# GpSimd computes the norm of the differential heads' outputs; VectorE keeps its sums over heads

## Chip, cores and metric

The kernel runs on one core of one Trainium2 chip. The metric is the device time of one execution in microseconds. The profile names the engines PE (TensorE matmul), DVE (VectorE), ACT (ScalarE), POOL (GpSimd) and SP (SyncE, here the DMA queue for weights).

## What is computed

Two transformer blocks of two layers each on 256 tokens of width 1024. The change lies in the attention of the first block, which runs once for each of its two layers. That layer has four kinds of heads; one of them, the differential heads, ends with a norm over each head's 64 outputs:

```python
def rmsnorm(x, g):
    xf = x.astype(jnp.float32)
    y = xf * lax.rsqrt(jnp.mean(xf * xf, axis=-1, keepdims=True) + EPS)
    return (y * g.astype(jnp.float32)).astype(x.dtype)
...
    out = from_blocks(lax.map(one_block, (to_blocks(q), jnp.arange(nb))))
    return rmsnorm(out, subln_g) * (1.0 - lam_init)
...
    mix = jnp.concatenate([o_a.reshape(b, s_len, -1), o_b.reshape(b, s_len, -1),
                           o_c.reshape(b, s_len, -1), o_d.reshape(b, s_len, -1)], axis=-1)
    x = x + rmsnorm(mix @ w_out, g_post_mix)
```

So the normed outputs of the differential heads (`o_c`) are a part of the left side of the product with `w_out`.

## The kernel before

Every engine has a program of its own, written out by hand in the order in which it shall run, and the engines meet at semaphores. The helpers `do` (DVE) and `step` (POOL) let an engine wait for each of its own instructions before the next one. All matmuls are made as three products of high and low parts of the operands, so each tile of weights that SP loads into `ring` gets a high part from ACT (`ring_hi`, L1652) and a low part from DVE (`ring_lo = ring - ring_hi`, L2166, or in two halves, L2174). The function `met` on DVE and ACT is where such a part is made.

The 256 tokens are two blocks of 128, `tb` 0 and 1. The attention of a layer is ten units, `u` 0 to 9: for each block c0, c1 (the differential heads, two and two), d (sliding), b (forgetting), a (selected keys). For a unit PE makes the logits two units ahead (`logits`, L1026, L1033, L1036), DVE the maxima (`maxima`, L2413 to L2418), ACT the exponentials (`exps`, L1739), PE transposes the probabilities (`prob_transposes`, L720 from ARENA) and ACT copies them out of PSUM (L1729), PE multiplies with the values (`values`, L1060), and DVE weighs the result into `XN` (`out`, L2444, L2445 or L2447), which raises the semaphore `o_ready`. The tile `SM` of the profile holds all small tensors (`ms8`, `r8`, `p_sub` and others), `ARENA` the scratch tensor `SQC`.

Behind unit c1 (u = 1 and 6) DVE's function `between` squares the four differential heads' 128x256 outputs, sums each head's 64 squares and adds the epsilon (L2452, L2453, L2454). POOL raises the four means to the power -1/2 (`asked`, L3048, 128x4). One unit later (u = 2 and 7) DVE multiplies the outputs by the root and by the gain `p_sub` (L2459, L2460) and raises `cd_ready`.

PE uses these outputs in `output_transposes(tb, 1)`, four transposes of `XN` columns 512 to 1023 (L720 from XN), which wait for `cd_ready`: for block 0 in unit 3, ahead of `last_columns(3, 1)` (the last products of the input projection), and for block 1 in unit 8, ahead of `values(8)`. ACT and DVE then split the transposed outputs (L1678, L2193), and `out_rows` multiplies them with `w_out`. In `between`, DVE also makes the selection mask (`choose`, L2367 to L2373) and in units 2 and 4 the low part of a weight tile.

POOL has little other work. At the start of the stage it rotates the heads c and d for both blocks (L3083 to L3086, L3117), then loads a gain vector (`gains`, a DMA issue, L3091), serves the two powers, and later serves the norms of the layer (L3052, L3048).

Of the kernel before, what the change touches and what calls it, by code (L numbers as in the profile page):

```python
# [12 lines left out]
ALU = mybir.AluOpType  # L13
ACT = mybir.ActivationFunctionType
AX_X = mybir.AxisListType.X

P = 128
D = 1024
S = 256  # L20
NTB = S // P
KT = D // P
DEPTH = 2
EPS = 1e-6
BIG = 1e30
TAKEN = -3e38
HD = 64
# [107 lines left out]
def build(nc, at, n_const, const_d, w, out_d):  # L135
    ctx = ExitStack()

    def sb(name, shape, dt=F32):
        return ctx.enter_context(nc.sbuf_tensor(name, shape, dt))

    def sig(name):
        return Signal(ctx.enter_context(nc.semaphore(name)))
# [24 lines left out]
    XN = sb("XN", [P, NTB, D])  # L167
# [22 lines left out]
    def c(name):  # L190
        o, n = at[name]
        return C[:, o:o + n]
# [4 lines left out]
    def small(n):  # L197
        o = small_at[0]
        small_at[0] += n
        assert small_at[0] <= 900  # L200
        return SM[:, o:o + n]
# [4 lines left out]
    p_sub = small(128).rearrange("p (l d) -> p l d", l=2)  # L206
# [16 lines left out]
    ms8, r8 = small(8), small(8)  # L223
# [4 lines left out]
    def ar(o, n):  # L228
        assert o + n <= ARENA_N, (o, n)
        return ARENA[:, o:o + n]  # L230
# [16 lines left out]
    SQC = ar(o + 896, 256)  # L247
# [131 lines left out]
    dstep, astep, pstep = sig("dve_step"), sig("act_step"), sig("pool_step")  # L379
    a2d, d2a = sig("act_to_dve"), sig("dve_to_act")  # L380
    d2p, p2d = sig("dve_to_pool"), sig("pool_to_dve")
# [5 lines left out]
    pv_done, o_ready = sig("pv_ready"), sig("o_ready")  # L387
# [5 lines left out]
    in_half = sig("last_columns_first_block")  # L393
    mask_made = sig("selection_mask")
    cd_ready = sig("differential_and_sliding_outputs")
    idx_s, idx_taken = sig("index_dots"), sig("index_dots_taken")
    silu_ready, hb_ready = sig("silu_ready"), sig("hidden_ready")
    h_full, h_side = sig("hidden_half_full"), sig("hidden_low_products_copied")
# [24 lines left out]
    def step(eng, ins, s):  # L423

        ins.then_inc(s.sem, 1)
        s.made += 1
        eng.wait_ge(s.sem, s.made)
# [169 lines left out]
    NU = len(UNITS)  # L597
# [33 lines left out]
    def half_bank(tb, half):  # L631

        return T[0] if half == 0 else G[:, 1, :] if tb else Sp[:, 0, :]
# [16 lines left out]
    def _(pe):  # L650
# [63 lines left out]
        def transposes(i, pairs, parts=False, act_takes=False, other=False):  # L714

            if not other:
                bank_free_t(i)
            for dst, src in pairs:
                k = src.shape[0]
                last = pe.transpose(dst, src, ident[0:k, 0:k])  # L720
            n = n_x if parts else n_p if act_takes else n_t
            n[i] += 1
            t_free[i] = (x_taken[i] if parts else p_taken if act_takes else t_taken[i], n[i])
            last.then_inc((x_full[i] if parts else p_full if act_takes else t_full[i]).sem, 1)
# [186 lines left out]
        for l in range(DEPTH):  # L911
# [151 lines left out]

            def output_transposes(tb, half):
                if half:
                    pe.wait_ge(cd_ready.sem, NTB * l + tb + 1)
                else:
                    pe.wait_ge(o_ready.sem, NU * l + NU // 2 * (tb + 1))
                bank = half_bank(tb, half)
                other = half == 1  # L1070
                kept = t_free[0]
                transposes(0, [(bank[:, k * P:(k + 1) * P], XN[:, tb, (4 * half + k) * P:(4 * half + k + 1) * P]) for k in range(4)], parts=True,
                           other=other)
                if other:
                    half_taken.append(t_free[0])
                    t_free[0] = kept
# [27 lines left out]
            for u in range(NU):  # L1104
                tb = UNITS[u][2]
# [142 lines left out]
        for l in range(DEPTH):  # L1248
# [99 lines left out]
            for lv in range(1, LEVELS):  # L1348
# [21 lines left out]
                if lv <= NTB:  # L1370

                    tb = lv - 1
# [255 lines left out]
        for h in range(2):  # L1628
            pe.wait_ge(z_l.sem, h + 1)
            cs = slice(h * 512, (h + 1) * 512)  # L1630
# [519 lines left out]
    def _(dve):  # L2150
        v = nc.vector
# [3 lines left out]
        def do(ins, s=None):  # L2155

            step(dve, ins, s or dstep)
# [21 lines left out]
        def met(n, ahead=H - 1):  # L2179

            n_use["dve"] += n
            low_parts(n_use["dve"] + ahead)
# [150 lines left out]
        for l in range(DEPTH):  # L2333
# [112 lines left out]
                else:  # L2446
                    do(v.tensor_tensor(dst, src, weights_, ALU.mult), o_ready)  # L2447

            def sublayer_squares(tb):
                oc = XN[:, tb, 512:768]  # L2450
                cs = slice(4 * tb, 4 * tb + 4)
                do(v.tensor_tensor(SQC, oc, oc, ALU.mult))  # L2452
                do(v.tensor_reduce(ms8[:, cs], SQC.rearrange("p (h n) -> p h n", h=4), AX_X, ALU.add))  # L2453
                do(v.tensor_scalar(ms8[:, cs], ms8[:, cs], 1.0 / HD, EPS, ALU.mult, ALU.add), d2p)  # L2454

            def sublayer_norm(tb):
                dve.wait_ge(p2d.sem, p2d.next("dve"))
                oh = XN[:, tb, 512:768].rearrange("p (h d) -> p h d", h=4)
                do(v.tensor_tensor(oh, oh, r8[:, 4 * tb:4 * tb + 4].unsqueeze(2).to_broadcast([P, 4, 64]), ALU.mult))  # L2459
                do(v.tensor_tensor(oh, oh, p_sub[:, l, :].unsqueeze(1).to_broadcast([P, 4, 64]), ALU.mult), cd_ready)  # L2460

            def low_evac_half(half, tb):
                ks, toks = slice(4 * half, 4 * half + 4), slice(tb * P, (tb + 1) * P)
                low_evac(0, xTl[:, ks, toks], xTh[:, ks, toks], half_bank(tb, half))

            def between(u):
                if u in (1, 6):
                    sublayer_squares(u // 5)
                if u in (2, 7):
                    sublayer_norm(u // 5)  # L2470
                if u == 3:
                    low_evac_half(1, 0)
                if u in LOW_AT:
                    met(1, LEAD)
                if u < len(CHOOSE_AT) and CHOOSE_AT[u]:
                    choose(1, sum(CHOOSE_AT[:u]), sum(CHOOSE_AT[:u + 1]))
# [138 lines left out]
        for l in range(DEPTH):  # L2615
# [148 lines left out]
            for lv in range(1, LEVELS):  # L2764
# [13 lines left out]
                if 2 <= lv <= NTB + 1:  # L2778

                    tb = lv - 2  # L2780
                    t0()
                    src = T[0][:, :].rearrange("p (h d) -> p h d", h=4)
                    cs = slice(4 * tb, 4 * tb + 4)
# [4 lines left out]
                if 3 <= lv <= NTB + 2:  # L2788

                    tb = lv - 3  # L2790
# [217 lines left out]
        for h in range(2):  # L3008
            cs = slice(h * 512, (h + 1) * 512)
# [31 lines left out]
    def _(pool):  # L3041
        g = nc.gpsimd
# [4 lines left out]
        def power(dst, src, n, s):  # L3047
            g.tensor_tensor(dst, src, c("mhalf")[:, 0:n], ALU.pow).then_inc(s.sem, 1)  # L3048
# [25 lines left out]
        def asked(dst, src, n, s_in=d2p, s_out=p2d):  # L3074
            pool.wait_ge(s_in.sem, s_in.next("pool"))
            power(dst, src, n, s_out)
# [11 lines left out]
        def gains(q, name, l):  # L3088

            vec_loaded[q].made += 16  # L3090
            pool.dma_start(VEC[:, q, :], w[name][l].partition_broadcast(P)).then_inc(vec_loaded[q].sem, 16)  # L3091

        def gains_loaded(q):
            pool.wait_ge(vec_loaded[q].sem, vec_loaded[q].made)
# [5 lines left out]
        for l in range(DEPTH):  # L3100
            if l:
                gains_loaded(1)
                rms()

                gains(0, "norm_post_mix", l)

            def rotated(col, heads, width, tb, s=None):
                cos, sin = (RCOS32, RSIN32) if width == 32 else (RCOS, RSIN)
                n = heads * width  # L3110
                rope(PROJ[:, tb, col:col + n], cos[:, tb, :], sin[:, tb, :], heads, width, XN[:, 1, 0:n], XN[:, 1, 256:256 + n], s)

            def sliding(tb):
                rotated(D_Q, 4, 64, tb)
                rotated(D_K, 2, 64, tb)
                for q, col in enumerate((D_K, D_K + 64)):
                    last = g.tensor_copy(IKD[:, 1 + q, tb, :].rearrange("p (r d) -> p r d", r=2),  # L3117
                                         PROJ[:, tb, col:col + 64].unsqueeze(1).to_broadcast([P, 2, 64]))
                last.then_inc(d_rotated.sem, 1)

            def differential(tb):
                rotated(C_Q, 8, 32, tb)
                rotated(C_K, 8, 32, tb, c_rotated)

            pool.wait_ge(g_act.sem, l * G_ACT + 10)
            differential(0)
            pool.wait_ge(g_act.sem, l * G_ACT + 11)
            sliding(0)
            differential(1)
            pool.wait_ge(g_act.sem, l * G_ACT + 13)  # L3130
            sliding(1)

            gains(1, "norm_pre_mlp", l)
            for tb in range(NTB):
                asked(r8[:, 4 * tb:4 * tb + 4], ms8[:, 4 * tb:4 * tb + 4], 4)
            for q in range(2):
                gains_loaded(q)
            rms_behind_rms()

            gains(0, "norm_post_mlp", l)  # L3140
            load(PLE, w["p"][l, 0].rearrange("(t p) d -> p t d", p=P), misc_loaded)
            gains_loaded(0)
            rms()

            gains(1, *(("norm_pre_mix", l + 1) if l + 1 < DEPTH else ("ln1_b_2", 0)))
            if l == DEPTH - 1:
                load(WSA, w["a_ws_2"][0].rearrange("g t s -> t g s"), misc_loaded)
        for l in range(DEPTH):
# [10 lines left out]
            for tb in range(NTB):  # L3159
                pool.wait_ge(o_ms.sem, o_ms.next("pool"))  # L3160
                cs = slice(4 * tb, 4 * tb + 4)
# [68 lines left out]
```

## Time and profile before

| | us |
|---|---|
| median of 3 runs | 2010.65 (2010.52 to 2013.17) |
| the profiled execution | 2010.38 |
| its span, first to last instruction | 2008.6 |
| PE busy | 1977.7 |
| DVE busy | 1582.2 |
| ACT busy | 1215.8 |
| POOL busy | 98.4 |

The profiled execution's own time is 1.8 us above its span. The stage of the change is 95 to 145 us from the span's start in layer 0, and ends at 497 in layer 1. A bracket at the end of a row of the timeline tells how long the engine was idle before that row, and which instruction's end let it go on.

### The profile page before, as it was taken

To read this page: it belongs to the slowest core of one execution; us is meant where nothing else is said; L and a number is where in the kernel's file an instruction comes from. 1 tells how busy PE (TensorE), PEld (TensorE's weight loads), DVE (VectorE), ACT (ScalarE), POOL (GpSimd) and SP (SyncE) were. 2 spreads that over 40 slices of the span, in tenths; PEclk is the share of its full clock that TensorE was granted. 3 is DMA by queue.
4 is the path that set the end of the run, shared out by engine and by line. 5 is a ranking of instruction groups with operands and counts; after the bars stand their busy time and mean duration, and the time that the engine had idled before them with its cause. 6 is when DMAs were issued, how large, how long until landed. Compare 5 with 4: busy or idle time off the path is not lost.

```text
span 2008.6 us, 30332 instructions
## 1 busy us (share of the span) xinstructions
PE 1977.7 (98%) x11699; PEld 1677.9 (84%) x11699; DVE 1582.2 (79%) x1634; ACT 1215.8 (61%) x1303; POOL 98.4 (5%) x163
## 2 busy tenths in 40 slices
PE   8999999999999999999999999999999999999997
PEld 7878888887888898888889888888888888888886
DVE  7787745778774569775548978999999998989997
ACT  6565534556553456544436636777777777777775
POOL 0300000030000000000000000000000000000000
PEclk9999999999999999999999999999999999999999
DMA  8326555632655554065556309999999999999995
GB/s 303 117 74 215 192 195 181 207 125 72 214 192 196 187 200 154 17 220 183 189 168 210 106 1 372 362 362 371 359 364 366 358 367 363 366 363 364 366 361 200
DMA packets 154088, 481.06 MB, mean 240 GB/s; under 512 B 14608, under 2 KB 41728, under 8 KB 153856
## 3 DMA queue, kind: packets, MB, share of 16 engines
q1 hardware_dynamic: 150064, 465.46, 64.1%
q0 software_dynamic: 3920, 14.16, 2.0%
q8 instruction: 73, 1.20, 0.2%
q14 instruction: 31, 0.25, 0.0%
HBM read 477.48 MB, written 2.10 MB: 239 GB/s over the span
## 4 chain that ended last, share of the span: by engine, by line
PE 89%; DVE 7%; ACT 2%; issue 1%; DMA 1%; POOL 0%; SPq 0%; DVEq 0%; POOLq 0%; ACTq 0%
PE G L693 18%; PE G L695 18%; PE G L694 18%; PE Sp L695 5%; PE Sp L693 5%; PE Sp L694 5%; PE G L1179 3%; PE G L720 3%; PE G L1180 2%; PE G L680 1%; DVE ring_lo L2166 1%; PE G L675 1%; PE G L676 1%; PE Sp L1179 1%; PE G L1567 1%
## 5 line engine op out<-in xcount | busy, mean ns | idle before, releaser
L2089 ACT ACTIVATE e_hi<-e_raw 128x1408 fp32r<-128x1408 f32 x384 | 523.4, 1380 | 156.9 <-DMA e_raw<-in_moe_w_gate 60.3
L2945 DVE TENSOR_TENSOR e_lo<-e_raw,e_hi 128x1408 fp32r<-128x1408 f32 x384 | 601.3, 1619 | 19.6 <-ACT e_hi L2089 17.2
L2166 DVE TENSOR_TENSOR ring_lo<-ring,ring_hi 128x2048 fp32r<-128x2048 f32 (+2 forms) x171 | 383.4, 2253 | 181.8 <-ACT ring_hi L1652 180.4
L1652 ACT ACTIVATE ring_hi<-ring 128x2048 fp32r<-128x2048 f32 (+1 forms) x179 | 335.4, 1882 | 228.9 <-PE G L695 137.1
L693 PE MATMUL G<-e_hi,xgTh 128*128 128x512 f32 (+1 forms) x768 | 289.2, 377 | 0.1
L695 PE MATMUL G<-e_hi,xgTl 128*128 128x512 f32 (+1 forms) x768 | 288.5, 376 | 0.0
L694 PE MATMUL G<-e_lo,xgTh 128*128 128x512 f32 (+1 forms) x768 | 287.1, 374 | 0.0
L693 PE MATMUL G<-ring_hi,xT 128*128 128x512 f32 (+2 forms) x488 | 190.9, 391 | 0.0
L695 PE MATMUL G<-ring_hi,xT 128*128 128x512 f32 (+2 forms) x488 | 187.4, 384 | 0.0
L694 PE MATMUL G<-ring_lo,xT 128*128 128x512 f32 (+2 forms) x488 | 187.2, 384 | 0.0
L694 PEld LDWEIGHTS G<-e_lo,xgTh 128*128 128x128 f32 x768 | 144.2, 188 | 23.9
L695 PEld LDWEIGHTS G<-e_hi,xgTl 128*128 128x128 f32 x768 | 144.0, 188 | 23.0
L693 PEld LDWEIGHTS G<-e_hi,xgTh 128*128 128x128 f32 x768 | 144.3, 188 | 22.6 <-DVE e_lo L2945 0.4
L693 PE MATMUL Sp<-e_hi,hEh 128*128 128x512 f32 x352 | 138.4, 393 | 0.0
L695 PE MATMUL Sp<-e_hi,hEl 128*128 128x512 f32 x352 | 137.4, 390 | 0.0
L694 PE MATMUL Sp<-e_lo,hEh 128*128 128x512 f32 x352 | 137.2, 390 | 0.0
L693 PEld LDWEIGHTS G<-ring_hi,xT 128*128 128x128 f32 x488 | 91.6, 188 | 19.3 <-issue 1.8
L695 PEld LDWEIGHTS G<-ring_hi,xT 128*128 128x128 f32 x488 | 91.6, 188 | 18.2
L694 PEld LDWEIGHTS G<-ring_lo,xT 128*128 128x128 f32 x488 | 91.7, 188 | 17.4 <-issue 0.5
L1179 PE MATMUL G<-xT,ring_hi 128*128 128x512 f32 x288 | 100.8, 394 | 0.0
L693 PE MATMUL G<-ring_hi,hTh 128*128 128x512 f32 x256 | 100.0, 391 | 0.0
L695 PE MATMUL G<-ring_hi,hTl 128*128 128x512 f32 x256 | 99.7, 389 | 0.0
(463 smaller groups left out, 3370.5 us busy)
## 6 DMA issues: line engine op xcount, KB each, us to landing
e_raw<-in_moe_w_gate SPq DMA_DIRECT2D x128, 704.0 KB, 6.0
e_raw<-in_moe_w_up SPq DMA_DIRECT2D x128, 704.0 KB, 6.0
e_raw<-in_moe_w_down SPq DMA_DIRECT2D x128, 704.0 KB, 6.0
ring<-in_w_in SPq DMA_DIRECT2D x48, 1024.0 KB, 4.9
ring<-in_w_mlp_up SPq DMA_DIRECT2D x32, 1024.0 KB, 5.1
ring<-in_w_mlp_down SPq DMA_DIRECT2D x32, 1024.0 KB, 4.8
ring<-in_w_out SPq DMA_DIRECT2D x16, 1024.0 KB, 4.8
ring<-in_ffn_w_gate SPq DMA_DIRECT2D x22, 512.0 KB, 3.6
```

The source lines that it names most:

```text
L675: pe.matmul(out, ah, bh, start=start, stop=False, **kw)
L676: return pe.matmul(out, al, bh, start=False, stop=False, **kw)
L693: pe.matmul(out, ah, bh, start=start, stop=False, **kw)
L694: pe.matmul(out, ah, bl, start=False, stop=False, **kw)
L695: return pe.matmul(out, al, bh, start=False, stop=stop, **kw)
L720: last = pe.transpose(dst, src, ident[0:k, 0:k])
L1179: pe.matmul(out.rearrange("p (w s) -> p w s", w=2), bh[:, k, ms_], xT[:, :, kk, :], start=kk == 0, stop=False, skip_group_check=True)
L1180: last = pe.matmul(out[:, 0:S], bl[:, k, ms_], xTh[:, kk, :], start=False, stop=kk == KT - 1, skip_group_check=True)
L1652: nc.scalar.activation(ring_hi[:, n % H, 0:m], ring[:, n % R, 0:m], ACT.Copy).then_inc(w_hi.sem, 1)
L2089: nc.scalar.activation(e_hi[:, u, :], e_raw[:, u, :], ACT.Copy).then_inc(w_hi.sem, 1)
L2166: v.tensor_tensor(ring_lo[:, n % R, cs], ring[:, n % R, cs], ring_hi[:, n % H, cs].bitcast(F32), ALU.subtract).then_inc(w_lo.sem, 1)
L2945: v.tensor_tensor(e_lo[:, u, :], e_raw[:, u, :], e_hi[:, u, :].bitcast(F32), ALU.subtract).then_inc(w_lo.sem, 1)
```

## The change

For each token block POOL now takes the squares, the mean with epsilon, the power and the two products, on its own; between the squares and the mean DVE sums the squares over each head. DVE's `sublayer_squares` and `sublayer_norm` go; `sublayer_sums` is called in units 2 and 7, behind `out` and `weigh`, and waits for the squares at the new semaphore `c_squared`. `cd_ready` is raised by POOL's last product. Since DVE's order no longer implies it, PE's `output_transposes(tb, 1)` also waits for the sliding heads' outputs at `o_ready`. POOL's four power requests per kernel (`asked`) become four calls of its `sublayer_norm`, in the same places of its program.

```diff
--- before.py
+++ after.py
@@ -393,6 +393,7 @@
     in_half = sig("last_columns_first_block")
     mask_made = sig("selection_mask")
     cd_ready = sig("differential_and_sliding_outputs")
+    c_squared = sig("differential_outputs_squared")
     idx_s, idx_taken = sig("index_dots"), sig("index_dots_taken")
     silu_ready, hb_ready = sig("silu_ready"), sig("hidden_ready")
     h_full, h_side = sig("hidden_half_full"), sig("hidden_low_products_copied")
@@ -1063,6 +1064,7 @@
 
             def output_transposes(tb, half):
                 if half:
+                    pe.wait_ge(o_ready.sem, NU * l + NU // 2 * tb + 3)
                     pe.wait_ge(cd_ready.sem, NTB * l + tb + 1)
                 else:
                     pe.wait_ge(o_ready.sem, NU * l + NU // 2 * (tb + 1))
@@ -2446,28 +2448,17 @@
                 else:
                     do(v.tensor_tensor(dst, src, weights_, ALU.mult), o_ready)
 
-            def sublayer_squares(tb):
-                oc = XN[:, tb, 512:768]
-                cs = slice(4 * tb, 4 * tb + 4)
-                do(v.tensor_tensor(SQC, oc, oc, ALU.mult))
-                do(v.tensor_reduce(ms8[:, cs], SQC.rearrange("p (h n) -> p h n", h=4), AX_X, ALU.add))
-                do(v.tensor_scalar(ms8[:, cs], ms8[:, cs], 1.0 / HD, EPS, ALU.mult, ALU.add), d2p)
-
-            def sublayer_norm(tb):
-                dve.wait_ge(p2d.sem, p2d.next("dve"))
-                oh = XN[:, tb, 512:768].rearrange("p (h d) -> p h d", h=4)
-                do(v.tensor_tensor(oh, oh, r8[:, 4 * tb:4 * tb + 4].unsqueeze(2).to_broadcast([P, 4, 64]), ALU.mult))
-                do(v.tensor_tensor(oh, oh, p_sub[:, l, :].unsqueeze(1).to_broadcast([P, 4, 64]), ALU.mult), cd_ready)
+            def sublayer_sums(tb):
+                dve.wait_ge(c_squared.sem, NTB * l + tb + 1)
+                do(v.tensor_reduce(ms8[:, 4 * tb:4 * tb + 4], SQC.rearrange("p (h n) -> p h n", h=4), AX_X, ALU.add), d2p)
 
             def low_evac_half(half, tb):
                 ks, toks = slice(4 * half, 4 * half + 4), slice(tb * P, (tb + 1) * P)
                 low_evac(0, xTl[:, ks, toks], xTh[:, ks, toks], half_bank(tb, half))
 
             def between(u):
-                if u in (1, 6):
-                    sublayer_squares(u // 5)
                 if u in (2, 7):
-                    sublayer_norm(u // 5)
+                    sublayer_sums(u // 5)
                 if u == 3:
                     low_evac_half(1, 0)
                 if u in LOW_AT:
@@ -3131,8 +3122,20 @@
             sliding(1)
 
             gains(1, "norm_pre_mlp", l)
+            def sublayer_norm(tb):
+                pool.wait_ge(o_ready.sem, NU * l + 5 * tb + 2)
+                oh = XN[:, tb, 512:768].rearrange("p (h d) -> p h d", h=4)
+                sq = SQC.rearrange("p (h d) -> p h d", h=4)
+                cs = slice(4 * tb, 4 * tb + 4)
+                g.tensor_tensor(sq, oh, oh, ALU.mult).then_inc(c_squared.sem, 1)
+                pool.wait_ge(d2p.sem, d2p.next("pool"))
+                step(pool, g.tensor_scalar(ms8[:, cs], ms8[:, cs], 1.0 / HD, EPS, ALU.mult, ALU.add), pstep)
+                step(pool, g.tensor_tensor(r8[:, cs], ms8[:, cs], c("mhalf")[:, 0:4], ALU.pow), pstep)
+                step(pool, g.tensor_tensor(oh, oh, r8[:, cs].unsqueeze(2).to_broadcast([P, 4, 64]), ALU.mult), pstep)
+                step(pool, g.tensor_tensor(oh, oh, p_sub[:, l, :].unsqueeze(1).to_broadcast([P, 4, 64]), ALU.mult), cd_ready)
+
             for tb in range(NTB):
-                asked(r8[:, 4 * tb:4 * tb + 4], ms8[:, 4 * tb:4 * tb + 4], 4)
+                sublayer_norm(tb)
             for q in range(2):
                 gains_loaded(q)
             rms_behind_rms()
```

On DVE, the stretch of layer 0 that runs from the reciprocal of unit 2 to the low part of the weights in unit 2, before (L2452 to L2454 are the squares, sums and mean, L2459 and L2460 the two products, MAX and MATCH_REPLACE belong to `choose`):

```order
L2425 TENSOR_TENSOR SM<-SM 128x4
L2426 RECIPROCAL SM<-SM 128x2x2
L2452 TENSOR_TENSOR ARENA<-XN 128x256
L2453 TENSOR_REDUCE SM<-ARENA 128x4
L2454 TENSOR_SCALAR SM<-SM 128x4
L2367 TENSOR_TENSOR ARENA<-ARENA,C 128x256
L2369 MAX SM<-ARENA 128x8
L2370 MATCH_REPLACE ARENA<-SM,ARENA 128x256
L2413 TENSOR_REDUCE SM<-G 128x4
L2418 TENSOR_SCALAR SM<-SM 128x4
L2447 TENSOR_TENSOR XN<-G,SM 128x256
L2426 RECIPROCAL SM<-SM 128x2x2
L2459 TENSOR_TENSOR XN<-XN,SM 128x256
L2460 TENSOR_TENSOR XN<-XN,SM 128x256
L2166 TENSOR_TENSOR ring_lo<-ring,ring_hi 128x2048
```

And in the changed kernel, whose line numbers are 2 higher here (L2453 is the sum over heads, L2168 the low part of the weights):

```order
L2427 TENSOR_TENSOR SM<-SM 128x4
L2428 RECIPROCAL SM<-SM 128x2x2
L2369 TENSOR_TENSOR ARENA<-ARENA,C 128x256
L2371 MAX SM<-ARENA 128x8
L2372 MATCH_REPLACE ARENA<-SM,ARENA 128x256
L2415 TENSOR_REDUCE SM<-G 128x4
L2420 TENSOR_SCALAR SM<-SM 128x4
L2449 TENSOR_TENSOR XN<-G,SM 128x256
L2428 RECIPROCAL SM<-SM 128x2x2
L2453 TENSOR_REDUCE SM<-ARENA 128x4
L2168 TENSOR_TENSOR ring_lo<-ring,ring_hi 128x2048
```

Five instructions are out of the stretch, and the sums stand directly ahead of the 128x2048 low part.

On POOL, what follows the last copies of the rotated heads in layer 0, before (L3048 is the power for both blocks):

```order
L3117 COPY AT_<-ARENA 128x128 x2
L3091 DMA VEC<-in_norm_pre_mlp 128x1024
L3048 TENSOR_TENSOR SM<-SM,C 128x4 x2
L3052 TENSOR_SCALAR SM<-SM 128x1
```

And in the changed kernel (L3130 squares, L3132 mean, L3133 power, L3134 and L3135 products, once for each block):

```order
L3108 COPY AT_<-ARENA 128x128 x2
L3082 DMA VEC<-in_norm_pre_mlp 128x1024
L3130 TENSOR_TENSOR ARENA<-XN 128x256
L3132 TENSOR_SCALAR SM<-SM 128x4
L3133 TENSOR_TENSOR SM<-SM,C 128x4
L3134 TENSOR_TENSOR XN<-XN,SM 128x256
L3135 TENSOR_TENSOR XN<-XN,SM 128x256
L3130 TENSOR_TENSOR ARENA<-XN 128x256
L3132 TENSOR_SCALAR SM<-SM 128x4
L3133 TENSOR_TENSOR SM<-SM,C 128x4
L3134 TENSOR_TENSOR XN<-XN,SM 128x256
L3135 TENSOR_TENSOR XN<-XN,SM 128x256
L3043 TENSOR_SCALAR SM<-SM 128x1
```

Two instructions have become ten, and each of them waits for the one ahead of it or for DVE.

On DVE in block 1 of layer 0, from the maxima of unit 9 to the low part of the transposed outputs (`low_evac_half(1, 1)`, L2193), before:

```order
L2413 TENSOR_REDUCE SM<-G 128x4
L2418 TENSOR_SCALAR SM<-SM 128x4
L2426 RECIPROCAL SM<-SM 128x2x2
L2174 TENSOR_TENSOR ring_lo<-ring,ring_hi 128x1024
L2447 TENSOR_TENSOR XN<-G,SM 128x256
L2459 TENSOR_TENSOR XN<-XN,SM 128x256
L2460 TENSOR_TENSOR XN<-XN,SM 128x256
L2426 RECIPROCAL SM<-SM 128x2x2
L2193 TENSOR_TENSOR xT<-G,xT 128x4x128
```

And in the changed kernel (L2195 is that low part):

```order
L2415 TENSOR_REDUCE SM<-G 128x4
L2420 TENSOR_SCALAR SM<-SM 128x4
L2428 RECIPROCAL SM<-SM 128x2x2
L2176 TENSOR_TENSOR ring_lo<-ring,ring_hi 128x1024
L2449 TENSOR_TENSOR XN<-G,SM 128x256
L2453 TENSOR_REDUCE SM<-ARENA 128x4
L2428 RECIPROCAL SM<-SM 128x2x2
L2195 TENSOR_TENSOR xT<-G,xT 128x4x128
```

The two products behind `out` of unit 7 (L2447) are gone, and the sums stand in their place. PE's order of instructions is the same in both kernels.

## Rows read from the trace of the kernel before

**Rows 1.** The page of the profile, busy time by engine (share of span, instructions)

```profile
PE 1977.7 (98%) x11699; PEld 1677.9 (84%) x11699; DVE 1582.2 (79%) x1634; ACT 1215.8 (61%) x1303; POOL 98.4 (5%) x163
```

**Rows 2.** Windows: busy time by engine (instructions), granted clock, DMA share, GB/s

```profile
100.00:145.00 45.00, 42.96 (x426) 34.40 (x425) 37.17 (x81) 30.53 (x82) 4.35 (x8) 1.00 0.18 60
452.00:497.00 45.00, 43.02 (x423) 34.63 (x424) 37.13 (x81) 29.85 (x80) 4.13 (x7) 1.00 0.18 60
```

**Rows 3.** Timeline of PE, layer 0: start, duration, line, tiles, count [idle before <-releaser]

```profile
100.48 0.69 PE L1060 MATMUL G<-ARENA 128*64 128x64 f32 x16 [0.26 <-DVE XN L2445]
...
106.59 0.60 PE L720 MATMUL Sp<-C,XN 128*128 128x128 f32 x4
...
112.00 0.47 PE L693 MATMUL Sp<-ring_hi,xT 128*128 128x512 f32 x1 [0.21 <-issue]
...
117.71 0.66 PE L720 MATMUL G<-C,ARENA 128*128 128x128 f32 x4 [0.73 <-ACT ARENA L1729]
118.52 0.50 PE L693 MATMUL Sp<-ring_hi,xT 128*128 128x512 f32 x1 [0.16 <-DVE ring_lo L2166]
...
123.32 0.63 PE L720 MATMUL G<-C,ARENA 128*128 128x128 f32 x4 [0.23 <-DVE xT L2193]
...
134.74 1.15 PE L1060 MATMUL G<-ARENA 128*64 128x64 f32 x32
...
138.18 0.60 PE L720 MATMUL G<-C,XN 128*128 128x128 f32 x4
```

**Rows 4.** Timeline of DVE, layer 0

```profile
99.77 0.56 DVE L2445 TENSOR_TENSOR XN<-AT_ 128x128 f32<-128x128 f32 x1
...
100.80 0.42 DVE L2452 TENSOR_TENSOR ARENA<-XN 128x256 f32<-128x256 f32 x1
101.25 0.42 DVE L2453 TENSOR_REDUCE SM<-ARENA 128x4 f32<-128x256 f32 x1
101.71 0.17 DVE L2454 TENSOR_SCALAR SM<-SM 128x4 f32<-128x4 f32 x1
101.91 0.43 DVE L2367 TENSOR_TENSOR ARENA<-ARENA,C 128x256 f32<-128x256 f32 x1
...
104.97 0.42 DVE L2459 TENSOR_TENSOR XN<-XN,SM 128x256 f32<-128x256 f32 x1
...
105.88 2.29 DVE L2166 TENSOR_TENSOR ring_lo<-ring,ring_hi 128x2048 fp32r<-128x2048 f32 x1
...
136.56 0.42 DVE L2447 TENSOR_TENSOR XN<-G,SM 128x256 f32<-128x256 f32 x1
```

**Rows 5.** Timeline of ACT, layer 0

```profile
115.24 0.47 ACT L1739 ACTIVATE ARENA<-G,SM 128x256 f32<-128x256 f32 x1 [2.77 <-DVE SM L2418]
```

**Rows 6.** Timeline of POOL, layer 0

```profile
101.97 1.28 POOL L3048 TENSOR_TENSOR SM<-SM,C 128x4 f32<-128x4 f32 x1 [0.65 <-DVE SM L2454]
133.78 1.01 POOL L3048 TENSOR_TENSOR SM<-SM,C 128x4 f32<-128x4 f32 x1 [30.54 <-DVE SM L2454]
```

**Rows 7.** Groups of POOL by line and shape: count, busy us, mean ns, idle before

```profile
L3086 POOL TENSOR_TENSOR ARENA<-XN 128x256 f32<-128x256 f32 x12 | 9.2, 766 | 0.9
L3048 POOL TENSOR_TENSOR SM<-SM,C 128x4 f32<-128x4 f32 x8 | 8.8, 1096 | 62.7 <-DVE SM L2454 62.4
...
L3162 POOL TENSOR_SCALAR SM<-SM 128x4 f32<-128x4 f32 x4 | 0.9, 230 | 215.5 <-ACT ARENA L2038 215.5
```

**Rows 8.** Timelines of DVE and POOL where the two engines meet

```profile
22.32 2.28 DVE L2166 TENSOR_TENSOR ring_lo<-ring,ring_hi 128x2048 fp32r<-128x2048 f32 x1
...
22.80 1.88 POOL L3052 TENSOR_SCALAR SM<-SM 128x1 f32<-128x1 f32 x1 [2.90 <-ACT ARENA L1753]
24.76 0.57 POOL L3048 TENSOR_TENSOR SM<-SM,C 128x1 f32<-128x1 f32 x1
...
336.75 2.29 DVE L2166 TENSOR_TENSOR ring_lo<-ring,ring_hi 128x2048 fp32r<-128x2048 f32 x1 [1.00 <-ACT ring_hi L1652]
...
337.80 1.32 POOL L3052 TENSOR_SCALAR SM<-SM 128x1 f32<-128x1 f32 x1 [11.10 <-ACT XN L1694]
```

## The prediction

> **What bounds the kernel now.** I read the page first: PE is busy 98% of the span, DVE 79%, POOL 5% [rows 1]. So time is lost or won only where PE waits. The windows put the stage of the change in numbers: of 45 us PE is busy 43.0, DVE 37.2, POOL 4.4, and layer 1 has the same sums to 0.3 us [rows 2]. PE idles some 2 us in each. The timeline of PE shows for what: 0.26 us for DVE's output of unit c1, 0.21 ahead of the first product with w_out, 0.73 for a copy by ACT, 0.16 for a low part and 0.23 for another [rows 3]. All five end at DVE, directly or through ACT: the copy stood behind ACT's exponentials of unit 6, which had idled 2.77 us for DVE's maxima [rows 5], and the 0.21 us, put down to "issue", is the wait for the low part of block 0's differential and sliding outputs. So between 96 and 123 us DVE sets PE's pace, and there a lighter DVE can be worth something. Then I looked at who uses the differential heads' outputs: PE's transposes at 106.59 and 138.18 us [rows 3], with no idle time ahead of either. DVE's second product ended ahead of 105.88 [rows 4], so the first margin is some 0.7 us; out(7) and two products of 0.46 each with its gap, from 136.56, leave the second some 0.25 us.
>
> **What the change removes.** On DVE, in block 0 the squares-sums-mean trio runs from 100.80 to the next instruction at 101.91, 1.11 us; the two products from 104.97 to 105.88, 0.91 us; the sums come back with 0.46 (0.42 and a gap of 0.04) [rows 4]. DVE is 1.56 us lighter per block, 6.2 us in the kernel. PE executes the same instructions. POOL gains squares, mean, power and two products.
>
> **The new path to the transposes.** Before, the power was asked for a unit ahead of the products, so its time lay beside DVE's other work. Now mean, power and both products follow the sums in a row, one waiting for the other. Prices: mean 0.23 (the 128x4 tensor_scalar), power 1.01 (the one of the two in this stage that nothing held; the mean of eight, 1.10, holds slowed ones), a 128x256 product 0.77 [rows 6, 7]. Between two of POOL's instructions, one waiting for the other, I take 0.08 (24.68 to 24.76) [rows 8]; from DVE's end to POOL's start 0.09 (101.88 to 101.97); from an output's end to PE's start 0.15 (100.33 to 100.48) [rows 3, 4, 6]. The 0.77 is that of the rotation's addition, whose shape is the products' but for their broadcast operand. The four take 0.23 + 1.01 + 0.77 + 0.77 and three gaps, 3.02 us.
>
> **Block 0.** DVE issues the sums at 105.88 - 1.56 - 0.46 = 103.86 us. POOL's squares aren't late: before the power at 101.97 it had idled 0.65 us, so it is free at 101.32 [rows 6], and ends them near 102.2. The sums end at 104.28, and DVE goes straight on with the 128x2048 low part, 104.32 to 106.61. Here I choose a price that decides much. A small tensor_scalar of POOL's takes 0.23 us [rows 7], but 1.88 and 1.32 us where it is issued while such a subtraction runs; these two ended at 24.68 and 339.12, the subtractions at 24.60 and 339.04 [rows 8]. The power at 101.97 took 1.28 rather than 1.01, and it was issued beside DVE's L2367, which also has two inputs in SBUF [rows 4, 6]. DVE wins the race by the rows: L2367 started 0.06 ahead. So POOL's mean ends at 106.69 instead of 104.60, the power at 107.78, the products at 108.63 and 109.48, and PE's transposes start at 109.63 rather than 106.59: **a stall of 3.04 us**. The Trainium skill bears on this: "GPSIMD Engine Reference", section Specifications, says that GpSimd's SBUF interfaces are shared with VectorE and contended by its instructions with two SBUF inputs. The trace agrees in the 1.88 us just named, and shows that it is a wait to the end, not a slowdown.
>
> Behind the waiting transposes on PE stand the last columns, logits(6) and the rest of the stage; ACT's and DVE's halves of these outputs wait too. But while PE stands DVE works on with what it has, and the four waits behind it go: 0.21 + 0.73 + 0.16 + 0.23 = 1.33 us [rows 3]. I checked the dearest: without its wait PE would have been there at 116.98, and is there at 120.0 now. The maxima of unit 6, which released ACT at 115.24 [rows 5], now follow PE's later logits instead of DVE's queue and end at about the same time, 115.4; four exponentials of some 0.45 us and the copy end near 118. A later wait of 0.33 us, for a copy by ACT in unit 7, stays, since ACT's own high part of a weight tile is ahead of it. Block 0 nets 3.04 - 1.33 = **1.71 us**.
>
> **Block 1.** Here DVE is not held by its own work: out(7) started at 136.56, and with 1.11 us less ahead of it waits for PE's values(7) instead, which end at 135.89 (134.74 + 1.15) [rows 3, 4]. From there to the transposes PE has 138.18 - 135.89 = 2.29 us of other work. The new chain is 0.15 to out(7), 0.42, a gap of 0.04, the sums 0.42, 0.09 to POOL, 3.02, 0.15 to PE: 4.29 us. DVE has only a reciprocal to do next and then waits for these transposes itself, so POOL isn't held. **The stall is 2.00 us**, and it stands relative to PE's own values(7), whatever block 0 did. Behind it I find no wait of PE in the stage that DVE's or ACT's earlier arrival would take away, so nothing comes back.
>
> **Sum.** 1.71 + 2.00 = 3.71 us a layer. Layer 1 has the same instructions and idle time in its window [rows 2], so twice: 7.4 us. The other stages are untouched, and with PE at 98% they absorb nothing. Made against the profiled execution, 2010.38 + 7.4 = 2017.8; that execution lies 0.3 us under the median of the runs shown, within their spread, and I add nothing. A measurement of this kernel tells about 0.2%, 4 us, from no change.
>
> **Bounds.** The lock: at nothing, POOL's mean runs beside the subtraction, block 0's stall is 0.96 us and the waits behind it still go, -0.37 net; the layer costs 1.6 and the kernel 3.3: 2013.6. The recovery: at nothing, 5.0 a layer, 10.1: 2020.5. A product on POOL lies between DVE's own 0.42 [rows 4], which would take 1.4 a layer away (2015.0), and the 1.10 of the power's mean [rows 7], which adds 1.3 a layer (2020.4); I take the row of the same shape. A power of 1.28 in both blocks adds 0.5 a layer.
>
> **Rivals.**
> 1. *POOL isn't held.* The mean slips in ahead of the 2.29 us subtraction. For it: the interval between them is 0.05 us, and DVE waits for its own semaphore as well. Against: L2367 won at 101.91. It gives 2013.6, and what is left is block 1's 2.00 us twice, less 0.7.
> 2. *The waits behind don't go.* The stall of 3.0 us delays maxima(6) and all behind it so that ACT's and DVE's chain stays as tight against PE as before. For it: PE's 3.0 us later logits are what the maxima wait for. Against: the copy has some 2 us in hand by my reckoning. It gives up to 2020.5.
> 3. *Not slower: DVE's relief is worth more than POOL's chain costs.* DVE is the pace of the stage up to 123 us, and every 1.56 us that it gains in block 0 could pull PE along. It decides once block 1's four instructions on POOL fit into what PE has in hand: 2.29 less the 1.27 us of handovers, out(7) and sums, so 1.02 us for all four, where the power alone takes 1.01. Its time, with no stall in block 1 and only the recoveries and an unheld POOL in block 0, is 2010.4 - 0.7 = 2009.7. The Trainium skill's "Perfetto Trace Analysis", section Optimizing Scalar/DVE Operations, holds both sides: offloading from a saturated VectorE may make sense, but because GpSimd shares its port it might not help. This trace has DVE at 37.2 of 45 us, and POOL's products at 0.77 against DVE's 0.42.
>
> **How the numbers follow.** The forecast's mechanism, stalls at both transposes with POOL held in block 0, gets 0.64, with its own range 2016 to 2019.5. POOL not held: 0.14, at 2013.6. Waits that stay or dearer POOL instructions: 0.16, at 2019.5 to 2021. Not slower: 0.06, half of it inside the 0.2%. The range from 2013.3 to 2020.8 takes in the first two and most of the third. Slower by over 0.2% means above 2014.7: 0.64 + 0.16 and nothing of rival 1, 0.80. Within 0.2%: rival 1's 0.14 and half of rival 3, 0.17. Faster: 0.03.
>
> **What the profile will show.** PE's transposes from XN (L721) with some 3 us of idle time in block 0 and 2 us in block 1, released by POOL; POOL's first mean near 2.3 us long and ending just behind DVE's low part, its second 0.23; the idle times of 0.73, 0.16 and 0.23 us gone; DVE's sums in block 0 without a wait; PE idle in the stage up from 2.0 to near 5.7 us in each layer. I am wrong if POOL's mean is short in block 0, if the copy's wait of 0.73 is still there, or if PE's idle time behind the transposes shrinks by more than those four waits. Granted clock: 1.00 in both windows [rows 2], with 0.7 us stalls in them; a fall of it behind a stall of 3 us would add to everything that I sum here.

## The result and the profile after

The changed kernel takes 2020.1 us (median of 6 runs, 2018.3 to 2021.4) against 2010.9 before (6 runs, 2010.5 to 2013.2): ratio 1.0045, 95% interval 1.0035 to 1.0055. That is 9.2 us slower, inside the range, 2.3 us above the forecast. The profiled execution took 2020.9 us.

The page of the changed kernel's profile, busy time by engine:

```profile
PE 1982.0 (98%) x11699; PEld 1681.1 (83%) x11699; DVE 1577.4 (78%) x1618; ACT 1215.6 (60%) x1303; POOL 111.1 (6%) x179
```

PE is busy 4.3 us longer with the same 11699 matmuls [rows 1]; that was not forecast. The windows of both layers' stages, then of three stretches of layer 0 (columns as in [rows 2]; the number ahead of the DMA share is the granted clock):

```profile
100.00:145.00 45.00, 40.45 (x372) 32.77 (x373) 33.98 (x72) 28.15 (x76) 9.46 (x13) 0.92 0.19 60
452.00:497.00 45.00, 41.64 (x386) 33.76 (x384) 37.70 (x80) 30.40 (x88) 12.17 (x20) 0.96 0.25 81
```

```profile
106.00:109.09 3.09, 0.44 (x4) 0.23 (x3) 2.95 (x7) 2.02 (x2) 2.71 (x4) 0.81 0.55 225
109.09:114.30 5.21, 5.21 (x21) 5.16 (x22) 2.95 (x9) 1.28 (x3) 0.00 (x0) 0.50 0.01 3
114.30:142.50 28.20, 26.84 (x247) 20.49 (x245) 21.70 (x43) 18.66 (x53) 2.93 (x5) 0.99 0.12 38
```

```profile
107.18 0.31 PE L694 MATMUL Sp<-ring_lo,xT 128*128 128x332 f32 x1
```

The timeline of PE in the changed kernel, layer 0 (L721 from XN are the transposes of [rows 3]):

```profile
109.09 1.08 PE L721 MATMUL Sp<-C,XN 128*128 128x128 f32 x4 [2.65 <-POOL XN L3135]
109.83 0.63 PE L694 MATMUL Sp<-ring_hi,xT 128*128 128x332 f32 x1
110.25 0.48 PE L695 MATMUL Sp<-ring_lo,xT 128*128 128x332 f32 x1
...
113.29 1.06 PE L721 MATMUL G<-C,ARENA 128*128 128x128 f32 x4
...
121.57 0.66 PE L721 MATMUL G<-C,ARENA 128*128 128x128 f32 x4
121.98 0.47 PE L694 MATMUL Sp<-ring_hi,xT 128*128 128x512 f32 x1
...
126.46 0.66 PE L721 MATMUL G<-C,ARENA 128*128 128x128 f32 x4
...
135.81 0.66 PE L721 MATMUL G<-C,ARENA 128*128 128x128 f32 x4 [0.20 <-ACT ARENA L1731]
...
137.78 1.15 PE L1061 MATMUL G<-ARENA 128*64 128x64 f32 x32
138.86 1.09 PE L721 MATMUL G<-C,ARENA 128*128 128x128 f32 x8
...
142.88 0.63 PE L721 MATMUL G<-C,XN 128*128 128x128 f32 x4 [1.54 <-POOL XN L3135]
```

Block 0's transposes waited 2.65 us for POOL's last product, block 1's 1.54. The waits of 0.73, 0.16 and 0.23 us behind block 0 are gone, and that of 0.33 has shrunk to 0.20. But the four transposes took 1.08 us, not 0.60, and the 128x332 products 0.48 each, not 0.31. Up to here the program ran 0.32 us earlier than in the profile before (values(2) at 100.16, not 100.48), so the transposes of block 0 came 2.82 us late, and those of block 1 5.02.

The timeline of POOL, both blocks of layer 0, and of DVE beside block 0:

```profile
101.03 0.62 POOL L3130 TENSOR_TENSOR ARENA<-XN 128x256 f32<-128x256 f32 x1
104.03 2.29 POOL L3132 TENSOR_SCALAR SM<-SM 128x4 f32<-128x4 f32 x1 [2.38 <-DVE SM L2453]
106.41 1.04 POOL L3133 TENSOR_TENSOR SM<-SM,C 128x4 f32<-128x4 f32 x1
107.53 0.61 POOL L3134 TENSOR_TENSOR XN<-XN,SM 128x256 f32<-128x256 f32 x1
108.22 0.72 POOL L3135 TENSOR_TENSOR XN<-XN,SM 128x256 f32<-128x256 f32 x1
...
139.94 0.20 POOL L3132 TENSOR_SCALAR SM<-SM 128x4 f32<-128x4 f32 x1 [3.75 <-DVE SM L2453]
140.22 1.01 POOL L3133 TENSOR_TENSOR SM<-SM,C 128x4 f32<-128x4 f32 x1
141.31 0.61 POOL L3134 TENSOR_TENSOR XN<-XN,SM 128x256 f32<-128x256 f32 x1
142.01 0.72 POOL L3135 TENSOR_TENSOR XN<-XN,SM 128x256 f32<-128x256 f32 x1
```

```profile
103.52 0.42 DVE L2453 TENSOR_REDUCE SM<-ARENA 128x4 f32<-128x256 f32 x1
103.98 2.29 DVE L2168 TENSOR_TENSOR ring_lo<-ring,ring_hi 128x2048 fp32r<-128x2048 f32 x1
```

In block 0 the 128x4 mean takes 2.29 us and ends at 106.32, right behind the subtraction (103.98 + 2.29 = 106.27); in block 1, with DVE idle, it takes 0.20. The two products take 0.61 and 0.72 us.

### The profile page after: what moved, and what is told of

The parts are those of the page before. It is cut to its first block, busy times and chain, and to the rows that moved or that the text cites. A ratio compares the mean times of both kernels' runs of the same rounds, so it can differ in the third digit from the quotient of the medians.

```text
span 2019.1 us, 30340 instructions
## 1 busy us (share of the span) xinstructions
PE 1982.0 (98%) x11699; PEld 1681.1 (83%) x11699; DVE 1577.4 (78%) x1618; ACT 1215.6 (60%) x1303; POOL 111.1 (6%) x179
## 4 chain that ended last, share of the span: by engine, by line
PE 90%; DVE 6%; ACT 2%; POOL 1%; issue 1%; DMA 1%; SPq 0%; POOLq 0%; DVEq 0%; ACTq 0%
PE G L694 18%; PE G L696 18%; PE G L695 18%; PE Sp L694 5%; PE Sp L696 5%; PE Sp L695 5%; PE G L1181 3%; PE G L721 3%; PE G L1182 2%; PE G L681 1%; PE G L676 1%; PE G L677 1%; PE Sp L1181 1%; PE G L1569 1%; DVE ring_lo L2168 1%
## 5 line engine op out<-in xcount | busy, mean ns | idle before, releaser
L2168 DVE TENSOR_TENSOR ring_lo<-ring,ring_hi 128x2048 fp32r<-128x2048 f32 (+2 forms) x171 | 383.4, 2253 | 183.3 <-ACT ring_hi L1654 182.0
```

The source lines that it names most:

```text
L2168: v.tensor_tensor(ring_lo[:, n % R, cs], ring[:, n % R, cs], ring_hi[:, n % H, cs].bitcast(F32), ALU.subtract).then_inc(w_lo.sem, 1)
```

## The experiments

Each change of a kernel is shown against the changed kernel, unless it says otherwise. Ratios are to the kernel before on the same chip, whose medians there were 2011.1, 2010.6 and 2010.9 us. The interval behind a ratio is some 2 us wide to each side, so smaller differences between two experiments are not told by their times alone.

**Is POOL's mean held by the subtraction?** The subtraction goes to unit 3:

```diff
-                if u == 3:
-                    low_evac_half(1, 0)
-                if u in LOW_AT:
+                if u in (3, 4):
                     met(1, LEAD)
+                if u == 3:
+                    low_evac_half(1, 0)
```

> The changed kernel with the 128x2048 low part of unit 2 moved on VectorE from directly behind the sums to unit 3, ahead of the low part of the transposed outputs. If GpSimd's mean was held by that subtraction, its mean in block 0 falls from 2.29 to about 0.2 us, PE's wait ahead of block 0's transposes from 2.65 to about 0.6 us, and the half clock behind it goes: about 2.0 us less stall and 1.5 to 2.6 us less of slow matmuls a layer, 2011 to 2013 us in all. If the mean is long by itself or the stall has another cause, nothing moves: 2020. If the half clock has nothing to do with the length of the wait, the clock still falls and the time is about 2016.

Measured: 2012.2 us, 1.0004 (0.9995 to 1.0014). POOL's chain of block 0:

```profile
104.16 0.19 POOL L3132 TENSOR_SCALAR SM<-SM 128x4 f32<-128x4 f32 x1 [2.38 <-DVE SM L2453]
104.44 1.04 POOL L3133 TENSOR_TENSOR SM<-SM,C 128x4 f32<-128x4 f32 x1
105.56 0.62 POOL L3134 TENSOR_TENSOR XN<-XN,SM 128x256 f32<-128x256 f32 x1
106.25 0.73 POOL L3135 TENSOR_TENSOR XN<-XN,SM 128x256 f32<-128x256 f32 x1
```

```profile
107.13 0.63 PE L721 MATMUL Sp<-C,XN 128*128 128x128 f32 x4 [0.56 <-POOL XN L3135]
```

The mean is 0.19 us, PE's wait 0.56 us, and the clock 1.00 in both windows. The kernel stands 1.2 us above the one before where the change stood 9.2: some 8 us hang on this one order, half of them the shorter wait (2.09 us, twice), the other half the clock, which the next runs price. The control is the same move in the kernel before:

> The kernel before with nothing but the move of the 128x2048 low part of unit 2 to unit 3. It is the control of the run that moved it in the changed kernel (2012.2). Theory: the move helps there only because GpSimd is freed, so here it gives nothing or costs up to 0.5 us a layer, since the low part of the transposed outputs comes later: 2011 to 2012. Rival: the move is a gain by itself, so that the other run does not speak of GpSimd: 2009 or less.

Measured: 2010.8 us, 0.9999 (0.9989 to 1.0008). The move alone gives nothing.

**What does the clock cost?** PE gets work for nothing while it waits:

```diff
                 if half:
+                    if tb == 0:
+                        turns(27, Sp[:, 0, :])
                     pe.wait_ge(o_ready.sem, NU * l + NU // 2 * tb + 3)
```

> The changed kernel with 27 transposes of the identity on PE, about 2.4 us of work for nothing, ahead of block 0's wait; the products that wait start no earlier. Theory: the idle 2.65 us let the clock fall to half, and that costs 2.6 us in layer 0 and 1.6 us in layer 1. Then the granted clock stays 1.00 in both stages and the time is 2015 to 2017 though PE starts block 0's transposes at the same moment. Rival: the low clock is a by-product with no price, or is not due to the idleness: 2019 to 2021.

Measured: 2016.4 us, 1.0027 (1.0017 to 1.0036). POOL's mean is still 2.29 us long, and the transposes start no earlier (9.05 us behind values(2), where it was 8.93: the 27 took 3.11 us, not 2.4, and overrun the wait by 0.12), but PE never idled ahead of them and its clock stayed up. The windows of the stage, and PE's rows at that place:

```profile
100.00:145.00 45.00, 43.00 (x418) 35.24 (x415) 34.72 (x72) 29.70 (x81) 9.89 (x14) 1.00 0.18 60
452.00:497.00 45.00, 43.03 (x435) 35.17 (x432) 36.23 (x77) 29.69 (x84) 11.55 (x18) 1.00 0.19 62
```

```profile
106.74 3.11 PE L909 MATMUL Sp<-C 128*128 128x128 f32 x27
109.68 0.60 PE L721 MATMUL Sp<-C,XN 128*128 128x128 f32 x4
110.04 0.40 PE L694 MATMUL Sp<-ring_hi,xT 128*128 128x332 f32 x1
```

This kernel is 5.3 us above the one before, the change 9.2. So work for nothing on PE saves 3.9 us: that is the price of the slow clock, as far as two measurements tell it, and the 5.3 are the stalls less what came back. With half as many transposes:

> The changed kernel with 13 instead of 27 transposes for nothing ahead of block 0's wait, so that PE idles some 1.5 us there instead of 2.65 or 0.2. Theory: the length of the idle time decides, so that the clock stays at 1.00 as behind the 1.54 us of block 1, and the time is that of the kernel with 27 (2016.4). Rival: block 0's place is more sensitive than block 1's: the granted clock falls behind it, and the time is 2018 or more.

Measured: 2015.7 us, 1.0025 (1.0015 to 1.0034). PE idled 1.25 us there and the clock stayed at 1.00:

```profile
109.18 0.63 PE L721 MATMUL Sp<-C,XN 128*128 128x128 f32 x4 [1.25 <-POOL XN L3137]
```

This kernel stands 4.8 us above the one before, so by it the slow clock costs 4.4 us. The traces say 4.1: from block 0's transposes to block 1's there are 31.22 us in layer 0 and 31.23 in layer 1 here, and 33.79 and 32.79 in the changed kernel. The rows show 2.65 us with a fall and 1.25 without; where between 1.54, the wait of block 1, and 2.65 it sets in was not tried.

**Which block?** With one block's norm as before (its squares, products and power on their old engines), the other's on POOL:

```diff
             for tb in range(NTB):
-                sublayer_norm(tb)
+                if tb == 0:
+                    sublayer_norm(tb)
+                else:
+                    asked(r8[:, 4 * tb:4 * tb + 4], ms8[:, 4 * tb:4 * tb + 4], 4)
```

> Only block 0's norm on GpSimd; block 1's as in the kernel before. Theory: the stall of 2.65 us and the slow clock are block 0's, the four small waits behind it are recovered: per layer 2.8 + 2.1 - 1.3 = 3.6 us, 2010.9 + 7 = 2018. Rival, with the price in both blocks alike: 2015.5.

Measured: 2016.0 us, 1.0025 (1.0014 to 1.0035), 2 us under what was expected. The runs reach from 2013.3 to 2019.9, and the time goes with the mean granted clock of the run: 2013.3 at 0.998, 2014.2 to 2015.0 at 0.997, 2017.1 and 2017.8 at 0.996, 2017.7 and 2019.9 at 0.995. The stretch at half clock differs from one time to the next though the wait is the same: in the profiled execution of this kernel (2014.5) it is 3.4 us in both layers, in that of the changed kernel 6.8 us in layer 0 and 3.4 in layer 1. The theory's sum was also too dear because it took only 1.3 us a layer for what comes back; it is 2.0, as shown below.

> Only block 1's norm on GpSimd; block 0's as in the kernel before. Theory: a stall of 1.5 us a layer, a full clock behind it, nothing recovered: 2010.9 + 3.1 = 2014. Rival, with the price in both blocks alike: 2015.5; rival, that a wait of 1.5 us also lowers the clock when it comes alone: 2016 or more.

Measured: 2014.8 us, 1.0018 (1.0008 to 1.0028), all ten runs within 1.5 us. PE's row for the waits of the whole kernel, then the window behind block 1's wait:

```profile
PE G L722 <- POOL XN L3156: 3.1, 2, 1.5
```

```profile
137.00:145.00 8.00, 6.46 (x63) 4.96 (x62) 1.02 (x2) 3.10 (x6) 2.24 (x4) 1.00 0.01 2
```

Two waits of 1.5 us, clock 1.00, 3.7 us. The two halves, 4.9 and 3.7, make 8.6 of the 9.2, which agrees within what can be told.

**Does the place matter for the clock?** Two more instructions in block 1's chain, on scratch that nobody reads:

```diff
+                if tb:
+                    for _ in range(2):
+                        step(pool, g.tensor_tensor(sq, sq, sq, ALU.subtract), pstep)
                 step(pool, g.tensor_tensor(oh, oh, r8[:, cs]
```

> The changed kernel with two more 128x256 products-like instructions (on scratch that nobody reads) in GpSimd's chain of block 1, some 1.4 us, so that PE's wait there grows from 1.54 to 2.9 us. Theory: a wait of this length lowers the clock wherever it stands; the granted clock behind block 1's transposes falls to 0.5 for some us, and the kernel takes 1.4 + 1.5 to 2.6 us more in each layer: 2026 to 2028. Rival: block 1's place keeps the clock up, and only the waits are added: 2023.

Measured: 2025.8 us (4 runs, 2023.7 to 2027.3), 1.0068 (1.0052 to 1.0085). The timeline of PE, and a window behind the wait:

```profile
144.42 0.63 PE L721 MATMUL G<-C,XN 128*128 128x128 f32 x4 [2.92 <-POOL XN L3138]
...
146.38 1.97 PE L721 MATMUL G<-C,ARENA 128*128 128x128 f32 x8
148.00 0.78 PE L694 MATMUL Sp<-ring_hi,xT 128*128 128x512 f32 x1
```

```profile
146.00:149.00 3.00, 3.00 (x20) 2.69 (x17) 0.91 (x2) 1.19 (x2) 0.00 (x0) 0.50 0.00 0
```

The clock falls here too, once the wait is 2.92 us. So it was the shorter wait, not block 1's place, that had kept it up. 1.4 us of added work per layer cost 2.8 us a layer, though with four runs that is a rough figure. The trace agrees: the wait is 1.38 us longer, and from the transposes to the values of unit 9 there are 7.02 us where the changed kernel has 5.43.

**What can VectorE's relief give?** The kernel before with the norm of these heads left out on all engines; the output transposes wait for `o_ready` alone:

> The kernel before with the differential heads' norm left out altogether (squares, sums, mean, power and products): VectorE is 2.0 us lighter per block and nobody waits for a norm. It prices what VectorE's relief can give back at most. Theory: the four small waits behind block 0 go, 1.3 to 1.5 us a layer: 2008.0. Rival: VectorE's relief is worth nothing to PE: 2011. Rival: PE had more in it than its waits show: under 2006.

Measured: 2006.8 us, 0.9979 (0.9969 to 0.9989). PE's waits of 0.21, 0.73, 0.16 and 0.23 us are gone and that of 0.33 is 0.22: 1.4 us of waits a layer by the brackets of the trace, 1.9 by the time, more than the theory had. The starts of PE's instructions settle which is right: from values(2) to block 1's transposes there are 35.64 us in layer 0 where the kernel before has 37.70, 2.06 less. A bracket counts from the modelled end of the instruction ahead, and in a stream without waits the next one starts before that end. The kernel before has 0.81 us from the transposes at 117.71 to the product at 118.52 and a bracket of 0.16; without the wait there are 0.41 (121.57 to 121.98 in the changed kernel). So that wait costs 0.40 us, not 0.16.

**What would have to be done to gain?** The sums are taken right behind the maxima:

```diff
                     maxima(u + 2)
+                if u in (2, 7):
+                    sublayer_sums(u // 5)
                 if u < 5:
                     out(u)
```

(and no more in `between`).

> The changed kernel with the sums taken directly behind the maxima (units 2 and 7) instead of behind the outputs; the 128x2048 low part stays in unit 2. Theory: GpSimd's mean and power then run ahead of the subtraction, and the subtraction holds whichever instruction comes next: the mean takes 0.2 us, the first product 1.5 instead of 0.6, block 0's transposes wait 1.2 to 1.5 us instead of 2.65 and the clock stays up, which gives back 3 us a layer; in block 1 the mean or the power is held by the 128x1024 low half (1.2 us), and the wait there is 0.5 to 1 us: 2012 to 2013 in all. Rival: only the mean, or only what is issued within the first 0.1 us, is held: block 0's wait is under 0.5 us, and the time 2010.

Measured: 2011.8 us, 1.0001 (0.9991 to 1.0010). POOL's chain in block 0 and the power in block 1, whose neighbour on DVE is a 128x1024 half from 133.99 to 135.21:

```profile
103.45 0.20 POOL L3132 TENSOR_SCALAR SM<-SM 128x4 f32<-128x4 f32 x1 [1.71 <-DVE SM L2453]
103.73 1.05 POOL L3133 TENSOR_TENSOR SM<-SM,C 128x4 f32<-128x4 f32 x1
104.85 1.98 POOL L3134 TENSOR_TENSOR XN<-XN,SM 128x256 f32<-128x256 f32 x1
106.91 0.73 POOL L3135 TENSOR_TENSOR XN<-XN,SM 128x256 f32<-128x256 f32 x1
...
134.11 1.97 POOL L3133 TENSOR_TENSOR SM<-SM,C 128x4 f32<-128x4 f32 x1
```

```profile
104.07 2.29 DVE L2168 TENSOR_TENSOR ring_lo<-ring,ring_hi 128x2048 fp32r<-128x2048 f32 x1
```

The hold moved to whichever instruction was issued next: the first product, 1.98 us, and in block 1 the power, 1.97. PE waited 1.27 us in block 0, with the clock at 1.00, and 0.26 in block 1, less than the 0.5 to 1 expected. With both moves:

> The changed kernel with both moves, sums behind the maxima and the low part in unit 3: the whole change as it stands, in both blocks, without a hold in block 0. Theory: no wait in block 0, and a wait of 0.5 to 1 us in block 1, where the 128x1024 low half holds GpSimd; VectorE's relief gives back 1.1 us a layer: 2010 to 2011. Rival: block 1's wait stays near 1.5 us: 2012.

Measured: 2010.4 us, 0.9995 (0.9985 to 1.0004). The wait at block 0 is gone, block 1's is 0.2 us, again less than expected. Last, only block 0 on POOL, with both moves:

> Block 0's norm on GpSimd with its sums taken directly behind the maxima of unit 2 and the 128x2048 low part moved to unit 3; block 1's norm as in the kernel before. Theory: GpSimd is not held and starts 0.7 us earlier, PE does not wait at block 0's transposes, block 1 costs nothing, and VectorE's relief of 1.6 us takes the four small waits away: 1.3 us a layer, 2008.5. Rival: the relief does not reach PE without the stall that let VectorE catch up: 2011.

Measured: 2009.7 us, 0.9993 (0.9984 to 1.0003), not to be told from no change. The same kernel again:

> The kernel with block 0's norm alone on GpSimd, early sums and the low part later, once more with more rounds, to tell its gain from nothing. By its trace PE lost 1.1 us of waits a layer, so 0.9990 of before and an interval that ends below 1, or, if that gain is spent elsewhere, 1.0000.

Measured: 2008.7 us (11 runs), 0.9988 (0.9979 to 0.9997). PE idles 0.95 us in layer 0's window, against 2.04 before:

```profile
100.00:145.00 45.00, 44.05 (x430) 35.34 (x429) 36.83 (x78) 30.26 (x82) 6.20 (x12) 1.00 0.18 60
452.00:497.00 45.00, 44.22 (x431) 35.59 (x431) 36.86 (x78) 29.69 (x80) 6.02 (x11) 1.00 0.18 60
```

The two measurements say 1.0 and 2.2 us faster, and only the second's interval leaves no change out. The starts on PE say 1.2 us a layer (36.50 and 36.51 us from values(2) to block 1's transposes in layer 0, against 37.70). It is a gain of 1 to 2 us at the edge of what can be told, from POOL taking only what fits.

## Why the prediction was right, and where it wasn't

*Direction and mechanism held.* Both transposes wait for POOL; the chain that lay beside other work now lies end to end between the sums and PE. The hold by the subtraction came as priced: the mean was forecast to end at 106.69 and ended at 106.32, with the whole program 0.32 us early. The Trainium skill's "SBUF — State Buffer", section Who interferes with whom, calls the pair of ports that VectorE and GpSimd share an exclusive lock, which the one who comes second waits for to the end; by that rule the trace agrees (1.98 and 1.97 us in the run with early sums, where 0.61 and 1.01 are needed). The first rival, that POOL isn't held, falls.

*The recovery came, and was priced too low.* The four waits behind block 0 went, 1.33 us by their brackets, and 0.13 more of the fifth, which I had counted as staying. So one of the signs of being wrong showed, that the idle time shrinks by more than those four. The starts on PE say more: from block 0's transposes to block 1's the half-filled kernel takes 31.22 us and the kernel before 31.59, though block 1's stall of 1.66 us is in the first; 2.03 us a layer came back, not 1.33. The second rival falls.

*The stalls were priced too high.* "A stall of 3.04 us" was a delay of 2.82, 2.65 of it idle. The other, "2.00 us", was 1.66: from values(7) to the transposes there were 3.44 us before (134.74 to 138.18) and are 5.10 now (137.78 to 142.88), 1.54 of them idle. Most of it is the products' price: 0.77 us each was taken from the rotation's addition, a mean of twelve that took 0.73 to 0.87, and the two measured 0.61 and 0.72, 0.2 us a chain; the other 0.1 of block 1 is in its handovers. Without the fall of the clock the kernel would have cost 4.8 us (half filled) or 5.3 (filled, with 0.24 us of overrun), where the sum said 7.4. With the measured terms the same sum is 2 x (2.82 + 1.66 - 2.03) = 4.9.

*The step that failed* is in "Block 0 nets 3.04 - 1.33 = 1.71 us": work behind the stall was counted at its old duration. The clock's fall was named in the last sentence as something that "would add to everything", with no price and no chance, because stalls of 0.7 us had left it at 1.00. It costs some 4 us of the 9.2 (3.9 and 4.4 by the two filled runs, 4.1 by the traces). In layer 0 of the profiled execution everything between 109.09 and 114.30 us ran at half clock: the twelve 128x332 products took 3.46 us from 109.83 to 113.29 instead of 1.92. So the forecast of 7.4 is near 9.2 by luck: stalls priced 1.1 us too high and a recovery priced 1.4 us too low stood in for a clock that was not priced.

*The third rival*, that VectorE's relief is worth more than POOL's chain costs, was given 6% for this change and is not what it does; but its premise is true. The relief is worth up to 3.8 us (norm left out), and two moves on DVE, and block 1's norm left where it was, keep a part of it.

What stays open: how far the idle time can go before the clock falls, beyond the rows above; and why the same wait of 2.65 us costs 6.8 us of half clock one time and 3.4 another.

## What to carry to other kernels

When work moves to an engine that shares a port with the one it leaves, look at what the first engine does directly behind the handover: here a 2.3 us subtraction held a 0.2 us instruction, and its place in the order decided 8 of 9.2 us. A stall on TensorE isn't priced by its length alone once it is long: ask at what clock the work behind it will run, and put that into the sum with a chance of its own. If such a stall can't be removed, work for nothing ahead of the wait buys the clock back. And price a wait on TensorE from start to start of the same instructions in two traces, not by its bracket: the brackets missed over a quarter of what came back here.

## What the runs showed of the hardware

TensorE's granted clock fell to 0.50 around a wait of 2.65 us in both layers and one of 2.92 us, and stayed at 1.00 around waits of 1.25, 1.27 (early sums) and 1.54 us. In layer 0 of the changed kernel it was down from 1.2 us ahead of the wait's end to 5.6 us behind it, in layer 1 for 3.4 us, from 0.4 us behind it. The runs of the kernel with block 0's norm alone spread over 6.6 us, but the changed kernel's spread over 3.1, and kernels without such a wait over 1.5 to 3.9, so the spread is no sure sign. The Trainium skill's "TensorE: Matmul & The Clock Gate", section Why this matters for your kernels, warns of idle gaps between bursts of matmuls; the trace agrees in that the clock fell around each of these longer waits. A window of layer 1:

```profile
466.00:469.50 3.50, 3.50 (x16) 3.50 (x17) 2.45 (x9) 0.60 (x1) 0.00 (x0) 0.54 0.02 7
```

GpSimd's 128x256 product with one operand broadcast along the inner axis took 0.61 us and with one broadcast along the heads 0.72, alike in every block where nothing held them (four of each in the changed kernel), 1.5 and 1.7 times VectorE's 0.42. A power of a 128x4 tile takes 1.01 to 1.05 us, longer than a 128x256 product.

VectorE can be the one held, too. In the changed kernel its 128x4 tensor_scalar behind the maxima of unit 5 fell beside POOL's second product (108.22 to 108.94 us) and took 0.55 us where it takes 0.17 elsewhere, in layer 1 as well:

```profile
108.42 0.55 DVE L2420 TENSOR_SCALAR SM<-SM 128x4 f32<-128x4 f32 x1
```
